# RWKV scan: backward cumulative sums by a reversed scan, backward inverse's second orientation by a mirrored TensorE product

## The chip, the cores and the metric

One core of one Trainium2 chip. The metric is the device time of one execution in microseconds (us), the median of several runs. All data are fp32.

## The reference

Two requests (1024 and 256 tokens, 1024 channels, 16 heads of 64) go through two layers with shared weights: neighbourhood attention with a gated feed-forward part, then bidirectional RWKV-7 time mixing with another. The change lies in the second mixer. In it, for each direction z (forward, and backward on the flipped sequence) and each head, a 64x64 state S runs over the tokens, and y of both directions is summed:

```python
def _wkv7_step(S, inp):
    r_t, w_t, k_t, v_t, aa_t, bb_t = inp
    sa = jnp.einsum('zbhij,zbhj->zbhi', S, aa_t)
    S = S * w_t[..., None, :] + sa[..., :, None] * bb_t[..., None, :] + v_t[..., :, None] * k_t[..., None, :]
    y = jnp.einsum('zbhij,zbhj->zbhi', S, r_t)
    return S, y
```

## The kernel before

The kernel is a sequence of stages, each with its own buffers and a barrier at its end. The change touches one of them, `rwkv_scan` (from about 2430 to 3440 us of the profile). It cuts the 1280 tokens into chunks of C = 64 and works in groups of U = 4 chunks, that is W = 256 tokens, for one pair of heads (128 partitions, one head on each half) and both directions z = 0 (forward) and z = 1 (backward). There are 8 pairs x 5 groups = 40 groups.

Within a chunk the recurrence becomes matrices. For each group: loads (SyncE); low-rank products (`lora`) and gates; running sums of the decay's logarithm over each chunk (`sums`, `sums_back`), exponentials of them on ScalarE (`exps`), keys and queries scaled by them on VectorE (`keys`, `queries`) and GpSimd (`directions`, `receptance`); products among them (`gram`), masked by VectorE (`strict_out`, `value_out`, `inclusive_out`); the inverse of a triangular 64x64 matrix for each chunk, head and direction; then the four steps of the state itself (`x_product`, `u_product`, `s_product`, each with a copy on ScalarE or, for the state, L2035 on VectorE), and the outputs (`y_products`).

**The sums.** For z = 0 a scan over the row, set to zero where a chunk begins by a multiplier `restart`, gives sums up to each token (L1910). For z = 1 the sums run from a chunk's end to each token: `sums` scans forward into `run` (L1911), and `sums_back` turns that round: it copies the chunk's total to column 0 (L1916) and subtracts the running sum from the total for the others (L1917). The semaphore `d_cum` then releases ScalarE's exponentials and GpSimd's L2085.

**The inverse** is built by doubling in levels 0 to 4 (INV = 5). Two matrices are held, `tf` and its transpose `rf`. A level is: product P of the masked matrix `bl` with `tf` (`level_p`, L1636) into `p_ps[z]`; a copy of it to `pt` by ScalarE (L1825); product T of `rf` and `pt` (`level_t`, L1647, last level L1649) into `t_ps[z]`; its sum with half of the columns of `tf` by VectorE (L2018); and then, so that `rf` follows, a VectorE transpose of the whole of `tf` in 32x32 blocks (L1993 for z = 0; L1995 for z = 1, in two instructions, because the backward inverse has the heads on swapped halves of the partitions in `rf`: `side(h, 1)` is the other half). The last level writes `rf` straight away (L2023).

Which half of the partitions a product reads and which it writes decides which quarter of the 128x128 array it works in. Forward P and T read and write the same half; backward P (`rows = halves[h]`, out `side(h, 1)`) and backward T, levels 0 to 3, read one half and write the other.

**The order** is written out by hand. Each engine runs, for I = -3 to 39, a loop over 12 slots n = 0 to 11; iteration I does the state's steps of group I, the inverse of group I + 1, the gram products of group I + 2 and the gates, sums and exponentials of group I + 3. In slot n of TensorE `inverse(I + 1, n)` does P of one direction and T of the other, interleaved chunk by chunk: in even slots 2k P forward of level k and T backward of level k - 1, in odd slots 2k + 1 P backward and T forward of level k:

```python
                    for s in range(U):
                        for h in range(2):
                            if does_p:
                                last_p = level_p(G, zp, k, s, h)
                        for h in range(2):
                            if does_t:
                                last_t = level_t(G, 1 - zp, kt, s, h)
```

State step products stand ahead of it: x, u and s in turn (n mod 3 = 0, 1, 2), and among them gram (n = 0, 1, 3, 6), lora (2), y of the group before (4, 5), turns of keys and values (7 to 10) and bonus (11). On VectorE a slot's order is: state (n = 2, 5, 8, 11), gram's masks, `level_out(I + 1, n)` (the sum and the transpose of the T product just made), and then the rest: `sums` in slot 3, `sums_back` in slot 4, `inverse_init` in 5 and 9, `keys` in 10, `queries` in 11. GpSimd runs its own row: masks of the levels (`levels`, L2117) for z = 0, then `directions` (L2085, L2087), which waits for `d_cum`, `receptance`, then the masks for z = 1. The program of every engine is written out in full for all 40 groups; there is no loop on the chip in this stage.

A 64x64 fp32 product leaves two records in the trace and two weight loads.

Of the kernel before, what the change touches and what calls it, by code (L numbers as in the profile page):

```python
# [15 lines left out]
ALU = mybir.AluOpType  # L16
# [3 lines left out]
P = 128  # L20
# [1360 lines left out]
C = 64  # L1381
# [7 lines left out]
def halves_of_level(t, z, k, other=False):  # L1389

    n = 2 ** (k + 1)
    return t.rearrange("p (b h n) -> p b h n", h=2, n=n)[:, :, (1 - z) if other else z, :]


def strided(a, off, dims):

    return bass.AP(tensor=a.tensor, offset=a.offset + off, ap=[list(a.ap[0])] + [list(d) for d in dims])


def rwkv_scan(nc, rkvl, kks, w0, w2, a0, a2, k_a, r_k, ysc, bsc, consts):  # L1400

    U = 4
    W = U * C
    NS = T // W
    NG = PAIRS * NS
    INV = LEVELS - 1
    halves = (slice(0, HD), slice(HD, P))
    with Phase(nc, "sc") as ph:
# [11 lines left out]
        restart = ph.sb("restart", [P, W])  # L1420
# [8 lines left out]
        sg = ph.sb("sg", [P, Z, W])  # L1429
# [2 lines left out]
        kd = ph.sb("kd", [P, Z, W])  # L1432
        ab = ph.sb("ab", [P, Z, W])
        cum = ph.sb("cum", [P, Z, W])
        run = ph.sb("run", [P, W])
        exb = ph.sb("exb", [P, Z, U, C + 1])
        ex2 = ph.sb("ex2", [P, Z, W])
        tb = ph.sb("tb", [P, Z, W])
# [9 lines left out]
        tf = ph.sb("tf", [P, 2, Z, U, C])  # L1448
        rf = ph.sb("rf", [P, 3, Z, U, C])
        r0 = ph.sb("r0", [P, U, C])  # L1450
        pt = ph.sb("pt", [P, Z, U, C])
# [14 lines left out]
        p_ps = [b[:, 0:256] for b in inv_ps]  # L1466
# [10 lines left out]
        a_tanh, a_sg, a_kdp, a_nega, a_ex1, a_ex2, a_x, a_u, a_fade = (  # L1477
            ph.sem(x) for x in ("a_tanh", "a_sg", "a_kdp", "a_nega", "a_ex1", "a_ex2", "a_x", "a_u", "a_fade"))
        a_pt, a_turn = ph.sems("a_pt", Z), ph.sems("a_turn", Z)
        d_start, d_cum, d_run, d_tb, d_rec, d_bonus, d_two, d_st, a_y = (  # L1480
            ph.sem(x) for x in ("d_start", "d_cum", "d_run", "d_tb", "d_rec", "d_bonus", "d_two", "d_st", "a_y"))
        d_bm, d_gram, d_first, d_t, d_r = (ph.sems(x, Z) for x in ("d_bm", "d_gram", "d_first", "d_t", "d_r"))
        g_kd, g_ab, g_r, g_bt = (ph.sem(x) for x in ("g_kd", "g_ab", "g_r", "g_bt"))
        g_bl, g_high, g_r0, g_first = (ph.sems(x, Z) for x in ("g_bl", "g_high", "g_r0", "g_first"))
# [7 lines left out]
        def group(G):  # L1492
            return 0 <= G < NG

        def side(h, z):
            return halves[h] if z == 0 else halves[1 - h]
# [8 lines left out]
        with nc.Block() as block:  # L1505
# [58 lines left out]
            def _(pe):  # L1564
# [74 lines left out]
                def level_t_waits(G, z, k):  # L1639
                    pe.wait_ge(a_pt[z], 5 * G + k + 1)  # L1640
                    if k:
                        pe.wait_ge(d_r[z], 4 * G + k)

                def level_t(G, z, k, s, h):
                    rows = side(h, z)
                    if k < INV - 1:
# [2 lines left out]
                    return nc.tensor.matmul(t_ps[z][rows, s * C:(s + 1) * C], pt_last[rows, z, s], rf[rows, G % 3, z, s],  # L1649
                                            start=True, stop=True)  # L1650

                def inverse(G, n):
                    if not group(G) or n > 2 * INV:
                        return
                    k, odd = divmod(n, 2)
                    zp = 1 if odd else 0
                    kt = k if odd else k - 1
                    does_p, does_t = k < INV, kt >= 0
                    if does_t:
                        level_t_waits(G, 1 - zp, kt)  # L1660
                    if does_p:
                        level_p_waits(G, zp, k)
                    for s in range(U):
                        for h in range(2):
                            if does_p:
                                last_p = level_p(G, zp, k, s, h)
                        for h in range(2):
                            if does_t:
                                last_t = level_t(G, 1 - zp, kt, s, h)
                    if does_p:  # L1670
                        last_p.then_inc(pe_p[zp], 1)
                    if does_t:
                        last_t.then_inc(pe_t[1 - zp], 1)

# [68 lines left out]
                for I in range(-3, NG):  # L1743
                    for n in range(3 * U):
                        s, part = divmod(n, 3)
# [144 lines left out]
            def _(dve):  # L1890
# [15 lines left out]
                def sums(G):  # L1906
                    dve.wait_ge(a_sg, G + 1)
                    if G >= 1:
                        dve.wait_ge(a_ex1, G)
                    nc.vector.tensor_tensor_scan(cum[:, 0], restart[:], sg[:, 0], 0.0, ALU.mult, ALU.add)  # L1910
                    nc.vector.tensor_tensor_scan(run[:], restart[:], sg[:, 1], 0.0, ALU.mult, ALU.add).then_inc(d_run, 1)  # L1911

                def sums_back(G):
                    dve.wait_ge(d_run, G + 1)
                    back, ahead = (t.rearrange("p (u n) -> p u n", n=C) for t in (cum[:, 1], run[:]))
                    nc.vector.tensor_copy(back[:, :, 0:1], ahead[:, :, C - 1:C])  # L1916
                    nc.vector.tensor_tensor(back[:, :, 1:C], ahead[:, :, C - 1:C].to_broadcast([P, U, C - 1]),  # L1917
                                            ahead[:, :, 0:C - 1], ALU.subtract).then_inc(d_cum, 1)

                def bonus_rows(G):  # L1920
                    p = G // NS
# [66 lines left out]
                def flat(t):  # L1988
                    return t.rearrange("p s n -> p (s n)")

                def turn_t(G, z):
                    if z == 0:
                        return nc.vector.transpose(flat(rf[:, G % 3, z]), flat(tf[:, G % 2, z]))  # L1993
                    for h, rows in enumerate(halves):
                        last = nc.vector.transpose(flat(rf[side(h, z), G % 3, z]), flat(tf[rows, G % 2, z]))  # L1995
                    return last

                def inverse_init(G, z):
                    dve.wait_ge(g_r0[z], G + 1)
                    if z == 0:  # L2000
                        nc.vector.transpose(flat(tf[:, G % 2, z]), flat(rf[:, G % 3, z])).then_inc(d_first[z], 1)
                        return
                    nc.vector.transpose(flat(tf[:, G % 2, z]), flat(r0[:])).then_inc(d_start, 1)
                    dve.wait_ge(d_start, G + 1)
                    if G >= 3:
                        dve.wait_ge(pe_u, 4 * G - 8)
                    turn_t(G, z).then_inc(d_first[z], 1)

                def level_out(G, n):
                    z = 1 - n % 2  # L2010
                    k = (n - 1) // 2
                    if not group(G) or not 0 <= k < INV:
                        return
                    dve.wait_ge(pe_t[z], 5 * G + k + 1)
                    if k < INV - 1:
                        src = halves_of_level(t_ps[z], z, k)
                        half = halves_of_level(flat(tf[:, G % 2, z]), z, k)
                        nc.vector.tensor_tensor(half, src, half, ALU.add).then_inc(d_t[z], 1)  # L2018
                        dve.wait_ge(d_t[z], 5 * G + k + 1)
                        turn_t(G, z).then_inc(d_r[z], 1)  # L2020
                    else:
                        half = rf[:, G % 3, z, :, (1 - z) * 32:(2 - z) * 32]
                        nc.vector.tensor_tensor(half, t_ps[z].rearrange("p (s n) -> p s n", s=U)[:, :, (1 - z) * 32:(2 - z) * 32], half, ALU.add).then_inc(d_t[z], 1)  # L2023

# [14 lines left out]
                for I in range(-3, NG):  # L2039
                    for n in range(3 * U):  # L2040
                        s, part = divmod(n, 3)
                        if group(I) and part == 2:
                            state_out(4 * I + s)
                        if n == 1 and group(I + 2):
                            strict_out(I + 2, 0)
                        if n == 2 and group(I + 2):
                            inclusive_out(I + 2, 0)
                        if n == 6 and group(I + 2):
                            strict_out(I + 2, 1)
                        if n == 7 and group(I + 2):  # L2050
                            inclusive_out(I + 2, 1)
                        level_out(I + 1, n)
                        if n == 0 and group(I + 2):
                            bonus_out(I + 2)
                        if n == 1 and group(I + 2):
                            value_out(I + 2, 0)
                        if n == 3 and group(I + 3):
                            sums(I + 3)
                        if n == 4 and group(I + 3):
                            sums_back(I + 3)  # L2060
                        if n == 5 and group(I + 2):
                            inverse_init(I + 2, 0)
                        if n == 6 and group(I + 2):
                            value_out(I + 2, 1)
                        if n == 8 and group(I + 3):
                            bonus_rows(I + 3)
                        if n == 9 and group(I + 2):
                            inverse_init(I + 2, 1)
                        if n == 10 and group(I + 3):
                            keys(I + 3)  # L2070
                        if n == 11 and group(I + 3):
                            queries(I + 3)
# [387 lines left out]
```

## Time and profile before

| | us |
|---|---|
| median of 3 runs | 4687.72 (4685.37 to 4695.64) |
| span of the profiled execution | 4696.3 |
| the profiled execution's own time | not listed apart from the three runs; the longest of them is 4695.64 |
| TensorE (PE) busy | 4245.7 (90%) |
| VectorE (DVE) busy | 1984.2 (42%) |
| ScalarE (ACT) busy | 1371.1 (29%) |
| GpSimd (POOL) busy | 1288.5 (27%) |

These are sums over all stages. PE is the product part of TensorE, PEld its weight loads, which overlap. The ends of products are modelled, so that a busy PE isn't one at its peak. The prediction reads the scan's steady part, 2560 to 3340 us, apart from the others.

### The profile page before, as it was taken

How to read it: one execution, taken by the hardware profiler on the slowest of the kernel's cores; microseconds unless marked ns; L12 is line 12 of the kernel's file. 1: busy time of each engine (PE TensorE's matmuls, PEld its weight loads, DVE VectorE, ACT ScalarE, POOL GpSimd, SP SyncE). 2: the span in 40 equal slices, each digit the busy share in tenths (PEclk: the TensorE clock that was granted, in tenths of full speed). 3: DMA queues.
4: the chain of work that ended last, by engine and by line, in shares of the span. 5: the costliest groups of instructions: out<-in, count | busy, mean ns of one | idle time of the engine just before them, and what ended most of it. 6: DMA issues, size and time to landing. Idle time of an engine off the chain costs nothing. (4 is left out here: it accounts for less than half of the span.)

```text
span 4696.3 us, 111143 instructions
## 1 busy us (share of the span) xinstructions
PE 4245.7 (90%) x49144; PEld 3578.0 (76%) x49144; DVE 1984.2 (42%) x3557; ACT 1371.1 (29%) x2872; POOL 1288.5 (27%) x882
## 2 busy tenths in 40 slices
PE   5999798999999997997958888888878999999997
PEld 5888666888888886775747777777756888888886
DVE  4111163253252442117227877887733253242441
ACT  2111274211110112236215555555522211111110
POOL 3111132311111124210116665665502311111110
PEclk8999899999999998998979999999988999999998
DMA  4122243312213112221232222222132312313114
GB/s 124 56 61 70 85 119 81 98 37 73 92 36 117 50 59 84 71 76 42 83 89 70 77 77 77 77 77 74 47 138 80 103 36 70 97 36 110 57 54 164
DMA packets 401484, 367.08 MB, mean 78 GB/s; under 512 B 62928, under 2 KB 370384, under 8 KB 398832
## 3 DMA queue, kind: packets, MB, share of 16 engines
q1 hardware_dynamic: 399568, 354.75, 24.6%
q8 instruction: 389, 6.37, 0.6%
q10 hardware_dynamic: 1440, 5.24, 0.3%
q14 instruction: 87, 0.71, 0.1%
HBM read 252.44 MB, written 107.48 MB: 77 GB/s over the span
## 5 line engine op out<-in xcount | busy, mean ns | idle before, releaser
L448 POOL TENSOR_TENSOR f_wlow<-f_raw,f_whigh 128x1024 fp32r<-128x1024 f32 (+1 forms) x152 | 360.4, 2371 | 1670.7 <-ACT f_whigh L519 1670.7
L504 PE MATMUL f_ps<-fx_hh,f_whigh 128*128 128x512 f32 (+1 forms) x2112 | 529.2, 359 | 0.0
L504 PE MATMUL f_ps<-fx_hl,f_whigh 128*128 128x512 f32 (+1 forms) x2112 | 528.2, 358 | 0.0
L504 PE MATMUL f_ps<-fx_hh,f_wlow 128*128 128x512 f32 (+1 forms) x2112 | 527.8, 358 | 0.0
L519 ACT ACTIVATE f_whigh<-f_raw 128x1024 fp32r<-128x1024 f32 (+1 forms) x152 | 156.5, 1030 | 922.1 <-PE f_ps L504 895.5
L504 PEld LDWEIGHTS f_ps<-fx_hl,f_whigh 128*128 128x128 f32 x2112 | 348.3, 188 | 66.2
L504 PEld LDWEIGHTS f_ps<-fx_hh,f_whigh 128*128 128x128 f32 x2112 | 348.2, 188 | 65.9
L504 PEld LDWEIGHTS f_ps<-fx_hh,f_wlow 128*128 128x128 f32 x2112 | 348.0, 188 | 66.1
L504 PE MATMUL f_ps<-mo_oh,f_whigh 128*128 128x512 f32 (+1 forms) x1440 | 361.0, 359 | 25.6 <-POOL f_wlow L448 25.6
L504 PE MATMUL f_ps<-mo_ol,f_whigh 128*128 128x512 f32 (+1 forms) x1440 | 360.4, 359 | 0.0
L504 PE MATMUL f_ps<-mo_oh,f_wlow 128*128 128x512 f32 (+1 forms) x1440 | 360.2, 358 | 0.0
L573 DVE TENSOR_TENSOR f_xo<-f_ps,f_xo 128x512 f32<-128x512 f32 x168 | 90.7, 595 | 618.8 <-PE f_ps L504 587.0
L1636 PE MATMUL sc_inv_ps<-sc_tf,sc_bl 64*64 64x64 f32 x6400 | 294.0, 226 | 26.6 <-issue 13.9
L2117 POOL TENSOR_TENSOR sc_bl<-sc_bm,sc_m_level 128x512 f32<-128x512 f32 (+1 forms) x160 | 245.7, 1557 | 231.3 <-DVE sc_pc L1940 231.3
L504 PEld LDWEIGHTS f_ps<-mo_oh,f_whigh 128*128 128x128 f32 x1440 | 240.5, 189 | 68.9 <-POOL f_wlow L448 26.2
L1636 PEld LDWEIGHTS sc_inv_ps<-sc_tf,sc_bl 64*64 64x64 f32 x6400 | 243.6, 135 | 47.3 <-issue 43.2
L504 PEld LDWEIGHTS f_ps<-mo_oh,f_wlow 128*128 128x128 f32 x1440 | 240.3, 188 | 42.8
L504 PEld LDWEIGHTS f_ps<-mo_ol,f_whigh 128*128 128x128 f32 x1440 | 240.1, 188 | 43.0
L1232 PE MATMUL ri_ps<-ri_xh,ri_whigh 128*128 128x512 f32 (+1 forms) x672 | 186.0, 387 | 74.5 <-DVE ri_xl L1348 73.5
L1647 PE MATMUL sc_inv_ps<-sc_pt,sc_rf 64*64 64x64 f32 x5120 | 228.5, 225 | 24.8 <-issue 24.7
L1647 PEld LDWEIGHTS sc_inv_ps<-sc_pt,sc_rf 64*64 64x64 f32 x5120 | 190.0, 136 | 26.6 <-issue 26.6
L594 DVE TENSOR_TENSOR f_gp<-f_ps,f_rs 128x1024 f32<-128x1024 f32 x44 | 53.9, 1226 | 357.0 <-PE f_ps L504 327.4
(267 smaller groups left out, 8482.2 us busy)
## 6 DMA issues: line engine op xcount, KB each, us to landing
f_xo<-xres SPq DMA_DIRECT2D x64, 640.0 KB
xres<-f_xo SPq DMA_DIRECT2D x56, 640.0 KB
f_raw<-in_ffn_w_gate SPq DMA_DIRECT2D x44, 512.0 KB
f_raw<-in_ffn_w_up SPq DMA_DIRECT2D x44, 512.0 KB
sc_rk<-rkvl SPq DMA_DIRECT2D x80, 256.0 KB
rkvl<-ri_ot SPq DMA_DIRECT2D x28, 640.0 KB, 2.9
f_raw<-in_ffn_w_down SPq DMA_DIRECT2D x32, 448.0 KB
qkv_raw<-in_na_w_qkv SPq DMA_DIRECT2D x24, 512.0 KB, 5.9
```

The source lines that it names most:

```text
L448: nc.gpsimd.tensor_tensor(wlow[:, m % 2, 0:kt], raw[:, 0:kt], whigh[:, m % 2, 0:kt].bitcast(F32), ALU.subtract).then_inc(cut_lo, 1)
L504: last = nc.tensor.matmul(ps[:, m % 2, n, 0:count], w[:, m % 2, k], x[:, k, t0:t0 + count], start=(k == 0 and w is whigh and x is xh), sto ...
L519: nc.scalar.activation(whigh[:, m % 2, 0:kt], raw[:, 0:kt], ACT.Copy).then_inc(cut_hi, 1)
L573: last = nc.vector.tensor_tensor(dst, src, old, ALU.add)
L594: nc.vector.tensor_tensor(gp[:, 1:1025], flat(s), rs[:, 0:1024], ALU.mult)
L1232: last = nc.tensor.matmul(ps[:, m % 2, q, 0:count], w[:, m % 2, k], src[:, k, t0:t0 + count], start=(k == 0 and w is whigh and src is xh), ...
L1636: return nc.tensor.matmul(p_ps[z][side(h, z), s * C:(s + 1) * C], bl[rows, G % 2, z, k, s], tf[rows, G % 2, z, s], start=True, stop=True)
L1647: return nc.tensor.matmul(t_ps[z][halves[h], s * C:(s + 1) * C], rf[rows, G % 3, z, s], pt[rows, z, s], start=True, stop=True)
L2117: nc.gpsimd.tensor_tensor(bl[:, G % 2, z, k:k + ks], src, mask, ALU.mult).then_inc(done[z], 1)
```

## The change

The sums of the backward direction are made by one scan that reads `sg[:, 1]` and writes `cum[:, 1]` from the last column to the first; both scans now stand in VectorE's slot 4. `run`, its semaphore, the copy and the subtraction go.

In the inverse, `rf` of the backward direction at levels 0 to 3 is no longer made by transposing `tf`. TensorE makes the transposed T product too: `level_mirrored` has the operands of `level_t` in the other order and writes the half from which it reads, into `p_ps[0]`, which is free in odd slots. It is interleaved with backward P one slot after that T (odd slots 3, 5, 7, 9), and the forward T products follow behind, by themselves. VectorE adds the result to half of the columns of `rf` (`mirrored_out`), which counts up `d_r[1]`; it stands behind the forward sum of that slot, or, at the last level, ahead of it.

```diff
@@ sums
-                    nc.vector.tensor_tensor_scan(run[:], restart[:], sg[:, 1], 0.0, ALU.mult, ALU.add).then_inc(d_run, 1)
-
-                def sums_back(G):
-                    dve.wait_ge(d_run, G + 1)
-                    back, ahead = (t.rearrange("p (u n) -> p u n", n=C) for t in (cum[:, 1], run[:]))
-                    nc.vector.tensor_copy(back[:, :, 0:1], ahead[:, :, C - 1:C])
-                    nc.vector.tensor_tensor(back[:, :, 1:C], ahead[:, :, C - 1:C].to_broadcast([P, U, C - 1]),
-                                            ahead[:, :, 0:C - 1], ALU.subtract).then_inc(d_cum, 1)
+                    back, ahead = (strided(t[:], 2 * W - 1, [[-1, W]]) for t in (cum, sg))
+                    nc.vector.tensor_tensor_scan(back, restart[:], ahead, 0.0, ALU.mult, ALU.add).then_inc(d_cum, 1)
@@ TensorE
+                def level_mirrored(G, s, h):
+                    rows = side(h, 1)
+                    return nc.tensor.matmul(p_ps[0][rows, s * C:(s + 1) * C], pt[rows, 1, s], rf[rows, G % 3, 1, s], start=True, stop=True)
...
-                    does_p, does_t = k < INV, kt >= 0
+                    does_p, does_t, does_mirrored = k < INV, kt >= 0, odd and k >= 1
...
                         for h in range(2):
-                            if does_t:
+                            if does_mirrored:
+                                last_p = level_mirrored(G, s, h)
+                            elif does_t:
                                 last_t = level_t(G, 1 - zp, kt, s, h)
                     if does_p:
                         last_p.then_inc(pe_p[zp], 1)
+                    if does_mirrored:
+                        for s in range(U):
+                            for h in range(2):
+                                last_t = level_t(G, 1 - zp, kt, s, h)
                     if does_t:
                         last_t.then_inc(pe_t[1 - zp], 1)
@@ VectorE
+                def mirrored_out(G, k):
+                    src = halves_of_level(p_ps[0], 1, k, True)
+                    half = halves_of_level(flat(rf[:, G % 3, 1]), 1, k, True)
+                    nc.vector.tensor_tensor(half, src, half, ALU.add).then_inc(d_r[1], 1)
...
                         nc.vector.tensor_tensor(half, src, half, ALU.add).then_inc(d_t[z], 1)
-                        dve.wait_ge(d_t[z], 5 * G + k + 1)
-                        turn_t(G, z).then_inc(d_r[z], 1)
+                        if z == 0:
+                            if k:
+                                mirrored_out(G, k - 1)
+                            dve.wait_ge(d_t[z], 5 * G + k + 1)
+                            nc.vector.transpose(flat(rf[:, G % 3, z]), flat(tf[:, G % 2, z])).then_inc(d_r[z], 1)
                     else:
+                        if z == 0:
+                            mirrored_out(G, k - 1)
...
-                        if n == 3 and group(I + 3):
+                        if n == 4 and group(I + 3):
                             sums(I + 3)
-                        if n == 4 and group(I + 3):
-                            sums_back(I + 3)
```

## Rows read from the trace of the kernel before

**Rows 1.** The page: span, then busy time of each engine, share, instructions.
```profile
span 4696.3 us, 111143 instructions
...
PE 4245.7 (90%) x49144; PEld 3578.0 (76%) x49144; DVE 1984.2 (42%) x3557; ACT 1371.1 (29%) x2872; POOL 1288.5 (27%) x882
```

**Rows 2.** Table by stretches, the scan's steady part; columns in the first line.
```profile
core 0: us, PE busy (x) PEld busy (x) DVE busy (x) ACT busy (x) POOL busy (x), PEclk, DMA share, GB/s
2560.00:3340.00 780.00, 659.07 (x24317) 605.36 (x24316) 621.00 (x1604) 441.57 (x1299) 467.68 (x414) 0.99 0.26 76
```

**Rows 3.** Waits of PE, 2560 to 3340 us: total, times, longest.
```profile
PE sc_inv_ps L1647 <- issue: 19.8, 20, 2.9
...
PE sc_chain_ps L1683 <- DVE sc_st L2035: 9.8, 23, 0.9
...
PE sc_inv_ps L1636 <- DVE sc_tf L2018: 4.9, 12, 1.2
...
PE sc_low_ps L1615 <- ACT sc_yt L1859: 3.5, 15, 0.2
```

**Rows 4.** Timeline of PE: start, duration, instruction, [idle before <- releaser].
```profile
2804.16 0.22 PE L1647 MATMUL sc_inv_ps<-sc_pt,sc_rf 64*64 64x64 f32 x1
2807.28 0.37 PE L1647 MATMUL sc_inv_ps<-sc_pt,sc_rf 64*64 64x64 f32 x1 [2.90 <-issue]
```

**Rows 5.** DMA queue 8 (packets, MB, share), 2560 to 3340, then 3025 to 3035.3.
```profile
q8 instruction: 193, 3.16, 1.7%
...
q8 instruction: 4, 0.07, 2.2%
```

**Rows 6.** POOL and DVE timelines: L2117 pair, four successive L1910; then all L1910 (ns, starts).
```profile
2997.63 3.04 POOL L2117 TENSOR_TENSOR sc_bl<-sc_bm,sc_m_level 128x512 f32<-128x512 f32 x2
...
2998.93 2.28 DVE L1910 TENSOR_TENSOR_SCAN sc_cum<-sc_restart,sc_sg 128x256 f32<-128x256 f32 x1 [0.17 <-ACT sc_sg L1796]
...
3022.20 2.29 DVE L1910 TENSOR_TENSOR_SCAN sc_cum<-sc_restart,sc_sg 128x256 f32<-128x256 f32 x1 [0.17 <-ACT sc_sg L1796]
...
3045.91 0.92 DVE L1910 TENSOR_TENSOR_SCAN sc_cum<-sc_restart,sc_sg 128x256 f32<-128x256 f32 x1 [0.17 <-ACT sc_sg L1796]
...
3069.53 0.92 DVE L1910 TENSOR_TENSOR_SCAN sc_cum<-sc_restart,sc_sg 128x256 f32<-128x256 f32 x1 [0.17 <-ACT sc_sg L1796]
...
L1910 DVE TENSOR_TENSOR_SCAN sc_cum<-sc_restart,sc_sg x33: 691/924/2299, 2568.3 to 3337.3; 128x256 f32<-128x256 f32 x33
```

**Rows 7.** Groups of DVE lines, 2560 to 3340: xcount | busy us, mean ns | idle.
```profile
L1995 DVE STREAM_TRANSPOSE sc_rf<-sc_tf 64x256 f32<-64x256 f32 x324 | 142.5, 440 | 7.7
...
L2018 DVE TENSOR_TENSOR sc_tf<-sc_inv_ps,sc_tf 128x128 f32<-128x128 f32 x260 | 74.6, 287 | 68.9 <-PE sc_inv_ps L1647 60.1
...
L1910 DVE TENSOR_TENSOR_SCAN sc_cum<-sc_restart,sc_sg 128x256 f32<-128x256 f32 x33 | 44.5, 1347 | 5.5 <-ACT sc_sg L1796 5.5
...
L1911 DVE TENSOR_TENSOR_SCAN sc_run<-sc_restart,sc_sg 128x256 f32<-128x256 f32 x33 | 21.8, 659 | 0.0
...
L1917 DVE TENSOR_TENSOR sc_cum<-sc_run 128x252 f32<-128x252 f32 x32 | 13.3, 414 | 0.0
...
L1916 DVE COPY sc_cum<-sc_run 128x4 f32<-128x4 f32 x32 | 5.5, 172 | 1.0
```

**Rows 8.** Timeline of PE: P and T interleaved, then a T alone.
```profile
2995.69 0.27 PE L1636 MATMUL sc_inv_ps<-sc_tf,sc_bl 64*64 64x64 f32 x2
...
2996.16 0.23 PE L1647 MATMUL sc_inv_ps<-sc_pt,sc_rf 64*64 64x64 f32 x2
2996.20 0.30 PE L1683 MATMUL sc_chain_ps<-sc_vt,sc_ga 64*64 64x64 f32 x8
...
2996.44 0.71 PE L1594 MATMUL sc_gram_ps<-sc_rec 64*64 64x128 f32 x10
...
3011.92 0.63 PE L1649 MATMUL sc_inv_ps<-sc_rf,sc_pt_last 64*64 64x64 f32 x16
3012.38 0.40 PE L1705 MATMUL sc_chain_ps<-sc_vt,sc_t 64*64 64x64 f32 x8
```

More of the change, by code:

```diff
@@ L1434, in rwkv_scan @@
         cum = ph.sb("cum", [P, Z, W])
-        run = ph.sb("run", [P, W])
         exb = ph.sb("exb", [P, Z, U, C + 1])
@@ L1479, in rwkv_scan @@
         a_pt, a_turn = ph.sems("a_pt", Z), ph.sems("a_turn", Z)
-        d_start, d_cum, d_run, d_tb, d_rec, d_bonus, d_two, d_st, a_y = (
-            ph.sem(x) for x in ("d_start", "d_cum", "d_run", "d_tb", "d_rec", "d_bonus", "d_two", "d_st", "a_y"))
+        d_start, d_cum, d_tb, d_rec, d_bonus, d_two, d_st, a_y = (
+            ph.sem(x) for x in ("d_start", "d_cum", "d_tb", "d_rec", "d_bonus", "d_two", "d_st", "a_y"))
         d_bm, d_gram, d_first, d_t, d_r = (ph.sems(x, Z) for x in ("d_bm", "d_gram", "d_first", "d_t", "d_r"))
@@ L1989, in flat @@
                     return t.rearrange("p s n -> p (s n)")
[L1991 to L1996, printed above, removed]
                 def inverse_init(G, z):
@@ L2006, in inverse_init @@
                         dve.wait_ge(pe_u, 4 * G - 8)
-                    turn_t(G, z).then_inc(d_first[z], 1)
+                    for h, rows in enumerate(halves):
+                        last = nc.vector.transpose(flat(rf[side(h, z), G % 3, z]), flat(tf[rows, G % 2, z]))
+                    last.then_inc(d_first[z], 1)
+                def mirrored_out(G, k):
+                    src = halves_of_level(p_ps[0], 1, k, True)
+                    half = halves_of_level(flat(rf[:, G % 3, 1]), 1, k, True)
+                    nc.vector.tensor_tensor(half, src, half, ALU.add).then_inc(d_r[1], 1)
                 def level_out(G, n):
```

## Prediction

> **What bounds the kernel now.** I read the page first [rows 1]: the span is 4696.3 us and TensorE is the busiest engine, but over stages of very different kinds. The change touches only the scan, so next came the table by stretches, cut to the scan's steady part [rows 2]: of 780 us TensorE is busy 659.07, VectorE 621.00 (80%), ScalarE 441.57, GpSimd 467.68. TensorE's clock is full there (0.99). Which engine sets the pace can't be read from 84% against 80%, so the third view was the waits of TensorE [rows 3]. Its idle time is 780 - 659.07 = 120.9 us. VectorE ends only 9.8 + 4.9 = 14.7 us of that, ScalarE 3.5; nearly all the rest, some 102 us, is "issue", idle time behind which no semaphore stands. One such stall is shown [rows 4]: in the middle of a row of identical products TensorE stops 2.90 us and then goes on.
>
> What is behind "issue" the DMA view tells [rows 5]: queue 8 brings instructions, 193 packets (3.16 MB, 16 KB each) in the 780 us, one each 780/193 = 4.04 us. The two halves of TensorE's work, products and weight loads, are 24317 + 24316 records in the same stretch [rows 2], 252 per packet: the packets are TensorE's own program, which is written out in full in this stage. In the densest stretch that I found, 10.3 us, four packets start; three intervals in about 10.3 us is 3.4 us each. Supply at its fastest is thus only some 15% above what the steady part draws. So two things bound this stage: the array's own time, and how quickly its instructions arrive. VectorE is busy, but TensorE seldom waits for it.
>
> A test of that is in the trace already [rows 6]. The forward scan of VectorE (L1910) takes 2.28 us where it starts while GpSimd multiplies at L2117 (from 2997.63 for 3.04 us), and 0.92 us elsewhere. This costs VectorE 1.4 us in two of five groups, and the groups don't feel it: after the two slow scans the next one starts 23.27 and 23.71 us later, after a quick one 23.62 us later. If VectorE set the pace, the first two would be over a microsecond longer.
>
> **The change part by part, per group of 4 chunks; the scan has 40.** In the steady part L1910 stands 33 times between 2568.3 and 3337.3 [rows 6]: 769.0/32 = 24.0 us a group.
>
> 1. *Removed, VectorE:* the eight 64x256 transposes of the backward inverse, two for each of its levels 0 to 3, 8 x 0.440 = 3.52 us [rows 7] (the 324 of that row are 10 a group; two belong to the start and stay). Forward transposes stay.
>
> 2. *Added, VectorE:* four sums `mirrored_out`, in operands like L2018's, 128x128 out of PSUM, 0.287 us [rows 7]: 4 x 0.29 = 1.15 us.
>
> 3. *Sums:* copy and subtraction go, about 0.17 + 0.41 us [rows 7], and the second scan stays but reads and writes backwards. No row shows a reversed scan. Bounds: as quick as the forward one, 0.659 us, and, as the bad end, 2.28 us as when the forward one met GpSimd. I take 0.66, being nearest in form. Both scans move one slot later, behind the backward sum of that slot and past the second L2117 multiply in most groups, so the 1.4 us collision should mostly go. VectorE altogether sheds 3.52 + 0.58 - 1.15 = 2.95 us a group, some 3.4 with the collision (the mean of L1910 is 1.347 us against a quick 0.92), 118 to 136 us over the stage. What waits for the sums is ScalarE's exponentials and GpSimd's L2085. The old chain ended with the subtraction in that same slot; two scans of 1.3 us take the place of transposes, copy and subtraction (0.89 + 0.58), so they end no later. I cost this at nothing; if it fails, GpSimd's slack before it is eaten first.
>
> The Trainium skill ("SBUF — State Buffer", the part on port contention) says that a VectorE instruction with two SBUF inputs and a GpSimd instruction that reads SBUF shut each other out for a whole instruction. The slow and the quick scan above agree with it; by it the subtraction's removal takes one more such meeting away, which changes VectorE's time only.
>
> 4. *Added, TensorE:* in slots 3, 5, 7, 9 eight 64x64 products `level_mirrored`, 32 a group, 1280 in all; each leaves two products and two weight loads in the records, 128 instructions a group. The price depends on which part of the array they occupy. In an odd slot today backward P reads one half of the partitions and writes the other, while forward T keeps to its own: the four quarters of the array work together. A timeline shows such a slot [rows 8]: 32 records from 2995.69, and x starts at 2996.20, 0.51 us. A set of 8 products that stands alone, backward T of the last level, has 16 records and the next product starts 12.38 - 11.92 = 0.46 us later [rows 8]. So half the work alone costs as much as two sets interleaved. In the new slot P is interleaved with the mirrored product, which keeps to its own half and so takes T's place beside P for free, and forward T follows by itself: +0.46 us in each of four slots, 1.84 us a group, 40 x 1.84 = 74 us. The other way to price it, by supply: 128 instructions are half a packet, at 3.4 us each 1.7 us a group, 68 us. The two aren't added: the lone T runs at a pace at which supply keeps up. Nor does "issue" time absorb it, as the slot draws both more time and more instructions. I take 74 and keep 0 (absorbed whole) and 2 x 74 = 148 (the mirrored product doesn't run beside P either) as outer bounds.
>
> The Trainium skill says otherwise on supply ("Runtime: NRT & Kernel Launch", Instruction fetch mechanics): crossing a 16 KiB boundary costs one DMA tail-bump, "mostly hidden". The 2.90 us stall speaks against that here. By that page the 68 us would be 0 and the 74 us of the array would stand alone.
>
> 5. *Moved and newly waited for:* backward R (`d_r[1]`) is done one slot later. In the following even slot TensorE waits for forward sum and then the mirrored sum, 0.29 us more than for the forward sum. Queued behind that wait are both products of the slot and all that follows. Cover: between the forward T and the next inverse step TensorE has x, y, gram or turn products, which hold it past that point (an x product takes 0.30 and half a gram 0.71 us [rows 8]); so nothing. If the cover is gone, 4 x 0.29 x 40 = 46 us. On VectorE the forward transpose and then the state (L2035) stand behind the new sum, 0.29 us later, but 0.89 us of transposes ahead of them are gone.
>
> 6. *Gained on TensorE:* at most what VectorE makes it wait, 14.7 us in 33 groups [rows 3], 18 for 40. I take 14, since the x products of slot 0 wait for a state that stands behind `keys`, which the change leaves.
>
> No DMA issue is added or moved on SP or GpSimd. **Sum:** +74 - 14 = +60 us. The profiled execution, 4696.3 us of span, would become 4756; it lies 8.6 us (0.2%) above the median of the runs shown, 4687.7, so the forecast is 4687.7 + 60 = 4748 us.
>
> **The rivals.**
> - *VectorE paces the scan after all* (faster). Place: the stretch from the scans to the state of slot 5, where its queue is fullest; it decides if the "issue" time is really a late VectorE. If a third of the 118 us that it sheds reaches the end and TensorE's addition runs in the cover, that is -40: 4648 us. For it: 80% busy. Against: 14.7 us of waits, and groups with slow scans are no longer. 0.14.
> - *The stalls absorb it.* 102 us of "issue" in the steady part is 3.1 us a group, more than the 1.84 added. If these stalls are fixed in time and not tied to how many instructions pass, the addition disappears in them, and 14 us may come back: 4674 to 4698, about 4688. The skill's page above would point here. Against: about six packets a group are drawn, and half a one more has to come too. 0.13.
> - *Dearer than costed.* The new wait of 5 decides as well, from the point at which the cover of 0.3 us is missing: 60 + 46 = +106, 4794 us; or the mirrored set doesn't pair with P, toward +134. Against: rows 8 show that pairing for the same halves. 0.11.
> - *Forecast:* 0.62.
>
> **How the numbers follow.** A measurement here can tell about 0.2%, 9 us. Faster takes the first rival and a little of the second: 0.16. Same is most of the second: 0.11. Slower: 0.73. The forecast's own range is +35 to +80, 4723 to 4768. For 8 in 10 I go down to the second rival's 4684 and up to 4782, part of the way to the dear case; left out are the faster case below and the rest of the dear one above.
>
> **What would show it.** Right: TensorE has 51704 product records in the whole kernel instead of 49144 (1280 x 2 more); VectorE some 118 us less busy; L1910's slow cases gone; the distance from scan to scan near 25.6 us instead of 24.0; 6.4 instruction packets a group; T records after P and mirrored ones, taking 0.46 us alone. Wrong: a distance of 24 us or less with "issue" shrunken; waits of the P product for `sc_rf` from the mirrored sum (the dear case); waits of L2085 grown beyond 102 us would show the sums late.

## The result, and the profile after

The changed kernel takes 4755.18 us (median of 4 runs, 4753.37 to 4755.74) against 4686.55 us, 68.6 us more: a ratio of 1.0142, interval 1.0129 to 1.0154. The forecast was 4748, in the range 4684 to 4782, with 0.73 on slower. The size came out. Why it is this size the prediction had only half right, and the experiments correct it.

The page after, its span and busy times:

```profile
span 4753.7 us, 116023 instructions
...
PE 4297.4 (90%) x51704; PEld 3637.5 (77%) x51704; DVE 1817.2 (38%) x3317; ACT 1373.3 (29%) x2872; POOL 1288.5 (27%) x882
```

Beside [rows 1]: 2560 more product records, as counted, and VectorE 1984.2 - 1817.2 = 167.0 us less busy. So VectorE lost more work than forecast, and the kernel became slower. The same stretch of the scan as in [rows 2], in the same columns, and then the packets of queue 8 (packets, MB, share), in that stretch and in the whole:

```profile
2560.00:3340.00 780.00, 662.91 (x24669) 616.54 (x24665) 451.03 (x1315) 415.38 (x1215) 439.51 (x390) 0.99 0.24 72
```

```profile
q8 instruction: 195, 3.19, 1.7%
...
q8 instruction: 409, 6.70, 0.6%
```

VectorE's 621.00 us have become 451.03. TensorE draws 195 packets of instructions in 780 us where it drew 193 [rows 5]: its program arrives as quickly as before, one packet each 4.0 us, but there is more of it. The kernel before drew 389 packets in all; 20 more for 40 groups are the half a packet a group of the prediction. How long a group takes can be read from the first of its scans, now L1919 (duration in ns min/median/max, first and last start), with the reversed one, L1921:

```profile
L1919 DVE TENSOR_TENSOR_SCAN sc_cum<-sc_restart,sc_sg x30: 680/681/1115, 2568.1 to 3315.7; 128x256 f32<-128x256 f32 x30
L1921 DVE TENSOR_TENSOR_SCAN sc_cum<-sc_restart,sc_sg x30: 658/666/669, 2568.7 to 3316.2; 128x256 f32<-128x256 f32 x30
```

747.6/29 = 25.78 us a group, against 24.03 [rows 6]: 1.75 us more, 70 us for 40 groups, all of the difference. The reversed scan costs what the forward one did (0.666 and 0.659 us), and the slow meetings with GpSimd are gone: the longest L1919 here is 1.115 us, where ten of the 33 in [rows 6] took 2.17 us or more.

The waits of TensorE (total, times, longest), and how VectorE's groups stand (xcount | busy us, mean ns | idle before, releaser):

```profile
PE sc_inv_ps L1635 <- issue: 18.6, 17, 1.7
PE sc_inv_ps L1646 <- issue: 15.0, 17, 2.3
...
PE sc_inv_ps L1653 <- issue: 10.3, 12, 1.9
...
PE sc_chain_ps L1692 <- DVE sc_st L2043: 4.8, 13, 0.4
```

```profile
L2021 DVE TENSOR_TENSOR sc_tf<-sc_inv_ps,sc_tf 128x128 f32<-128x128 f32 x244 | 71.3, 292 | 224.6 <-PE sc_inv_ps L1646 216.9
...
L2010 DVE TENSOR_TENSOR sc_rf<-sc_inv_ps,sc_rf 128x128 f32<-128x128 f32 x121 | 34.3, 284 | 42.3 <-PE sc_inv_ps L1648 42.3
```

TensorE's waits for VectorE shrank from 14.7 us [rows 3] to 4.8. VectorE now stands idle 216.9 us ahead of the sums of T (L2021) until TensorE's products are there; ahead of L2018 it was 60.1 [rows 7]. The relieved engine waits over three times as long as before for the one that took the work.

A slot with the mirrored products, in a timeline of TensorE: L1635 is P, L1653 the mirrored product, L1646 the forward T, L1706 the u product of the next slot.

```profile
2901.42 0.22 PE L1653 MATMUL sc_inv_ps<-sc_rf,sc_pt 64*64 64x64 f32 x2
2901.44 0.27 PE L1635 MATMUL sc_inv_ps<-sc_tf,sc_bl 64*64 64x64 f32 x2
2901.47 0.28 PE L1653 MATMUL sc_inv_ps<-sc_rf,sc_pt 64*64 64x64 f32 x4
...
2901.88 0.57 PE L1646 MATMUL sc_inv_ps<-sc_pt,sc_rf 64*64 64x64 f32 x14
2902.24 0.27 PE L1706 MATMUL sc_chain_ps<-sc_xs,sc_rf 64*64 64x64 f32 x2
```

The mirrored products run among the P products in the time that T had, and T follows alone: 0.36 us until the next slot's product begins, against the 0.46 reckoned (in most slots of the stage it is between 0.36 and 0.47).

### The profile page after: what moved, and what is told of

Same layout as the page of the kernel before. It is cut to its first block and busy times, and to the rows that moved or that the text cites. A ratio compares the mean times of both kernels' runs of the same rounds, so it can differ in the third digit from the quotient of the medians.

```text
span 4753.7 us, 116023 instructions
## 1 busy us (share of the span) xinstructions
PE 4297.4 (90%) x51704; PEld 3637.5 (77%) x51704; DVE 1817.2 (38%) x3317; ACT 1373.3 (29%) x2872; POOL 1288.5 (27%) x882
## 5 line engine op out<-in xcount | busy, mean ns | idle before, releaser
L1635 PE MATMUL sc_inv_ps<-sc_tf,sc_bl 64*64 64x64 f32 x6400 | 295.7, 226 | 25.5 <-issue 22.8
L1635 PEld LDWEIGHTS sc_inv_ps<-sc_tf,sc_bl 64*64 64x64 f32 x6400 | 244.0, 135 | 41.5 <-issue 38.2
L1646 PE MATMUL sc_inv_ps<-sc_pt,sc_rf 64*64 64x64 f32 x5120 | 224.4, 224 | 19.6 <-issue 19.6
L2021 DVE TENSOR_TENSOR sc_tf<-sc_inv_ps,sc_tf 128x128 f32<-128x128 f32 x320 | 93.4, 292 | 292.3 <-PE sc_inv_ps L1646 282.8
L1646 PEld LDWEIGHTS sc_inv_ps<-sc_pt,sc_rf 64*64 64x64 f32 x5120 | 186.6, 135 | 23.1 <-issue 23.1
```

Source lines behind the costliest of these rows:

```text
L1635: return nc.tensor.matmul(p_ps[z][side(h, z), s * C:(s + 1) * C], bl[rows, G % 2, z, k, s], tf[rows, G % 2, z, s], start=True, stop=True)
L1646: return nc.tensor.matmul(t_ps[z][halves[h], s * C:(s + 1) * C], rf[rows, G % 3, z, s], pt[rows, z, s], start=True, stop=True)
```

## The experiments

The theory was that TensorE pays, in array time or in supply of instructions; the rivals were that VectorE sets the pace, and that the new wait costs. Each kernel is compared with the kernel before on the same chip (medians 4701.29, 4698.20 and 4705.36 in the three sets).

### The parts of the change, each alone

**Sums alone** (the reversed scan in slot 4, the inverse as before):

```diff
-                    nc.vector.tensor_tensor_scan(run[:], restart[:], sg[:, 1], 0.0, ALU.mult, ALU.add).then_inc(d_run, 1)
...
+                    back, ahead = (strided(t[:], 2 * W - 1, [[-1, W]]) for t in (cum, sg))
+                    nc.vector.tensor_tensor_scan(back, restart[:], ahead, 0.0, ALU.mult, ALU.add).then_inc(d_cum, 1)
```

> The kernel before with the reversed scan a slot later, the inverse as before. TensorE's own time pays (theory): VectorE loses about 1.0 us a group (0.59 us of copy and subtraction, 0.43 us of collisions with GpSimd) and the end hardly moves: 0 to -8 us, 4678 to 4687. VectorE paces the scan (rival): a third or more of the 40 us that VectorE sheds comes through, -13 us or beyond, below 4674. The later sums hurt (rival): the exponentials and L2085 start late, +9 us or more.

Measured: 4698.71 against 4701.29 us, 0.9990 (0.9979 to 1.0001). VectorE is 42 us less busy by the page (1941.9), and nothing that can be measured comes through.

**Inverse alone** (the changed kernel with the sums of before):

```diff
+                def sums_back(G):
+                    dve.wait_ge(d_run, G + 1)
...
-                        if n == 4 and group(I + 3):
+                        if n == 3 and group(I + 3):
                             sums(I + 3)
+                        if n == 4 and group(I + 3):
+                            sums_back(I + 3)
```

> The changed kernel with the old sums. TensorE pays (theory): nearly the whole difference stands here, +60 to +80 us against the kernel before, 4746 to 4767. If the moved sums were the cause (rival), this kernel is within 15 us of the kernel before.

Measured: 4772.25 against 4701.29 us, +71.0, 1.0152 (1.0136 to 1.0168). The whole price is in the inverse. Against the 1.0142 of the whole change the sums give back 0.1% of the time, which lies inside the intervals.

**Relief alone** (VectorE spared the backward transposes, TensorE's work the same):

```diff
-                    if k:
+                    if k and z == 0:
                         pe.wait_ge(d_r[z], 4 * G + k)
...
-                        turn_t(G, z).then_inc(d_r[z], 1)
+                        if z == 0:
+                            turn_t(G, z).then_inc(d_r[z], 1)
```

> The kernel before without the transposes of the backward inverse at levels 0 to 3 (L1995, 8 of its 10 a group) and without TensorE's wait for them: the backward matrix R is left at its first value, so the inverse of the backward direction is another. TensorE's products stay as many. Theory: VectorE sheds 3.5 us a group, 141 us, and the end gains only what TensorE waits for VectorE, 5 to 18 us: 4668 to 4681. VectorE paces (rival): -40 us or more, below 4647.

Measured: 4694.40 against 4701.29 us, -6.9, 0.9987 (0.9978 to 0.9996), at the near end of the theory. VectorE is 130.9 us less busy over the kernel (1984.2 to 1853.3 by the pages), and 7 us of that arrive. The rival in which VectorE sets the pace, -40 us or more, is out.

**Products alone** (as many products as the change adds, in the same places and on the same halves, but from constants, so that nothing new is waited for; VectorE keeps its work):

```diff
+                def level_mirrored(G, s, h):
+                    rows = side(h, 1)
+                    return nc.tensor.matmul(p_ps[0][rows, s * C:(s + 1) * C], m_level[rows, 0, 0], ident[rows, rows], start=True, stop=True)
...
+                            if does_mirrored:
+                                last_p = level_mirrored(G, s, h)
...
+                    if does_mirrored:
+                        for s in range(U):
+                            for h in range(2):
+                                last_t = level_t(G, 1 - zp, kt, s, h)
```

> The kernel before with 32 products more a group in the places and the array half of the mirrored ones, from constants, their result unused, and forward T alone behind them as in the change. VectorE keeps all its work. Theory: the whole price without VectorE's relief, +70 to +90 us, 4756 to 4777, at or above the changed kernel. Rival (the price is the new wait for the mirrored sum, which is absent here): under +35 us.

Measured: 4766.27 against 4701.29 us, +65.0, 1.0137 (1.0121 to 1.0152), 5 us under the band. It is not the new wait: without it nearly the whole price is there. By this kernel and relief alone, inverse alone should be +58; it is +71. The 13 us between may be the new wait or the spread of layout and runs (the intervals are 7 us to either side); this is not settled.

**The change as a whole, again**, with the kernels of the last set, so that they share a chip:

> The changed kernel itself, beside the others of this set on one chip: +64 to +73 us against the kernel before, as measured first. It stands here so that it can be compared with the kernel of small added products, which costs 61.

Measured: 4773.71 against 4705.36 us, +68.4, 1.0142 (1.0127 to 1.0158).

### Array time or supply

Both prices of the prediction's step 4 gave about 70 us, so their sizes can't tell them apart. **Small** adds 32 products of 8 columns a group, **wide** adds 8 of 256 columns, both in slots 3, 5, 7, 9 ahead of P and T:

```diff
+                    if odd and k >= 1:
+                        for s in range(U):
+                            for h in range(2):
+                                nc.tensor.matmul(p_ps[0][halves[h], s * C:s * C + 8], ident[halves[h], halves[h]], m_level[halves[h], 0, 0, 0:8],
+                                                 start=True, stop=True)
```

```diff
+                    if odd and k >= 1:
+                        for h in range(2):
+                            nc.tensor.matmul(p_ps[0][halves[h], 0:256], ident[halves[h], halves[h]],
+                                             m_level[halves[h], 0:2].rearrange("p a z n -> p (a z n)"), start=True, stop=True)
```

> The kernel before with 32 products of 8 columns more a group in slots 3, 5, 7, 9 (128 instructions), ahead of P and T, which stay interleaved; results unused. Array time is paid (theory A): 8 columns cost an eighth of 64, some 0.06 us a slot at most, under +15 us. Instruction supply is paid (theory B): half a packet a group at 3.4 us, +50 to +70 us, as much as the change. Both bind in turn: in between, 20 to 45.

> The kernel before with two products of 256 columns more in each of the same slots, one on each half: the array time of eight 64-column ones (0.43 to 0.46 us a slot) with a quarter of their instructions (32 a group). Array time is paid (theory A): +60 to +74 us. Supply is paid (theory B): an eighth of a packet a group, 0.4 us, +10 to +25 us. Both in turn: in between.

Measured: small 4759.09 against 4698.20 us, +60.9, 1.0133 (1.0117 to 1.0148); wide 4717.49, +19.3, 1.0039 (1.0025 to 1.0053). What each puts into a slot, from timelines of TensorE, small first:

```profile
2903.68 0.41 PE L1666 MATMUL sc_inv_ps<-sc_m_level,sc_ident 64*64 64x8 f32 x10
...
2904.06 0.20 PE L1666 MATMUL sc_inv_ps<-sc_m_level,sc_ident 64*64 64x8 f32 x1
```

```profile
2899.08 0.38 PE L1665 MATMUL sc_inv_ps<-sc_m_level,sc_ident 64*64 64x256 f32 x1
...
2899.09 0.38 PE L1665 MATMUL sc_inv_ps<-sc_m_level,sc_ident 64*64 64x256 f32 x1
...
2899.30 0.38 PE L1665 MATMUL sc_inv_ps<-sc_m_level,sc_ident 64*64 64x256 f32 x2
...
2899.51 0.22 PE L1649 MATMUL sc_inv_ps<-sc_rf,sc_pt_last 64*64 64x64 f32 x2
```

The expectation of small was wrong in one point: products of 8 columns are not an eighth as dear. Sixteen records start from 2903.68 to 2904.06, each about as far from the next as those of 64 columns; their weight loads are as long as ever (135 ns). So small doesn't separate array time from instructions by itself. The pair does: both kernels keep their quarters of the array for about 0.4 us a slot (0.38 and 0.43), and they differ in instructions, 128 and 32 a group. The price follows the instructions: 61 and 19 us. At small's rate 32 instructions cost 61/4 = 15 us, which leaves wide 4 us for 4 x 0.43 x 40 = 69 us of array time. Array time is nearly free here, because TensorE is waiting for its program in any case. The steady part of wide, in the columns of [rows 2], shows where it goes:

```profile
2560.00:3340.00 780.00, 687.00 (x24133) 628.76 (x24133) 599.17 (x1560) 429.26 (x1265) 455.64 (x406) 0.99 0.25 74
```

TensorE is 27.9 us longer busy than before with nearly as many records, and its "issue" time fell from 100.4 to 82.4 us: the wide products fill time in which it stood idle.

That "issue" time is a wait for instructions can be read from the traces themselves. From 2560 to 3340 us of the changed kernel TensorE has 94 gaps of more than 0.5 us in which neither a product nor a weight load runs. Every one ends between 1.0 and 1.75 us after the landing of the last packet of queue 8 before it (median 1.39); with a packet each 4.0 us chance would put about one gap in five there. In small it is 98 of 98, in wide 70 of 70, in the kernel before 81 of 89, and in the kernel with one product of y, where VectorE holds TensorE up (below), 39 of 81. The distance from one packet's start to the next is not even: in the steady part of the kernel before it goes from 3.3 to 7.0 us, with 3.9 in the middle. What sets it, no run here shows.

**Twice as many small products**: the same edit with `for s in range(2 * U)`.

> Twice as many 8-column products in each of slots 3, 5, 7, 9: 256 instructions a group more than the kernel before. If how many instructions TensorE gets sets the pace (supply), the price doubles from the 61 us of 128: +115 to +130 us, and the packets in 780 us stay near 193. If the 61 us came from something that happens once a slot (a wait, the order of P behind other products, a switch of bank), it stays near 61, under 80.

Measured: 4855.08 against 4705.36 us, +149.7, 1.0318 (1.0304 to 1.0332). More than twice, so it is nothing that happens once a slot; the band was too low. The 28 us above twice 61 aren't explained; the clock of the stretch was 0.97 here and 0.99 before, which may be a part of them. The scan of this kernel and its packets, 2560 to 3340 us:

```profile
L1915 DVE TENSOR_TENSOR_SCAN sc_cum<-sc_restart,sc_sg x27: 691/693/1379, 2584.7 to 3314.9; 128x256 f32<-128x256 f32 x27
```

```profile
q8 instruction: 192, 3.15, 1.7%
```

730.2/26 = 28.08 us a group, 4.05 us more than before for one packet more. That is one packet at the mean distance, 780/192 = 4.06 us, and not at the 3.4 of the densest stretch. By the measured times, over all 40 groups, a packet costs 60.9/20 = 3.0 us in small and 149.7/40 = 3.7 us here.

**Fewer**: y from two of its three products, and from one. The first leaves the values' own part out of y, the second also the part of the state's corrections; all else is done.

```diff
-                                nc.tensor.matmul(y_ps[side(h, z), z, to[z]], tu[rows, g, z], nr[rows, G % 4, z, 0, s], start=False, stop=False)
-                        for h, rows in enumerate(halves):
-                            for z in range(Z):
-                                last = nc.tensor.matmul(y_ps[side(h, z), z, to[z]], vt[rows, G % 2, z, s], nr[rows, G % 4, z, 1, s], start=False, stop=True)
+                                last = nc.tensor.matmul(y_ps[side(h, z), z, to[z]], tu[rows, g, z], nr[rows, G % 4, z, 0, s], start=False, stop=True)
```

> The kernel before without the third of the three products that make y (the values' own part), 16 products and 64 instructions a group fewer, 0.25 packets. Supply: -30 us (-22 to -35), by 61 us for 128 instructions. Array time (16 products in four quarters, 0.23 us a group): -9 us. VectorE paces: 0 to -5.

> The kernel before with one of the three products of y, 128 instructions a group fewer: the change's addition with the other sign. Supply, still alone: -55 to -65 us, 4640. Supply until VectorE, which keeps all its work (19 us busy a group of 24), takes over as the next limit: -35 to -50. Array time: -18 us.

Measured: two products 4677.56 against 4705.36 us, -27.8, 0.9939 (0.9925 to 0.9952); one product 4661.03, -44.3, 0.9907 (0.9892 to 0.9922). The first 64 instructions give 28 us, in supply's band and three times the array time of those products. The next 64 give 16.5. What has taken over, the waits of TensorE and the packets of the kernel with one product tell:

```profile
PE sc_inv_ps L1636 <- DVE sc_tf L2012: 34.7, 39, 2.2
PE sc_chain_ps L1683 <- DVE sc_st L2029: 34.1, 51, 0.9
PE sc_low_ps L1724 <- issue: 5.9, 6, 1.9
```

```profile
q8 instruction: 183, 3.00, 1.6%
```

VectorE now ends 68.8 us of TensorE's idle time, where it was 14.7 [rows 3], "issue" has shrunk from 100.4 to 31.2 us, and packets come more rarely than they could, 183. With two products it is 34.8 and 75.5 us: VectorE comes in as the next limit step by step, within 44 us of the kernel before. That the work which this change takes from VectorE would be worth something below that point follows from it, but no run shows it.

### An attempt to use it

Transposes of `turn` for the lower half of the partitions were issued as transposes (the other stages' form, one record and one weight load each) in the hope of 48 instructions a group fewer; once alone, once with the sums:

```diff
+                def turned(out, a, rows):
+                    if rows.start == 0:
+                        return nc.tensor.transpose(out, a, ident[rows, rows])
+                    return nc.tensor.matmul(out, a, ident[rows, rows], start=True, stop=True)
```

> The kernel before with the turns of keys and values on the lower half of the partitions issued as transposes, one product record and one weight load instead of two of each, so 24 x 2 = 48 instructions a group fewer; the upper half, at its side in the array, is as before. Supply binds (theory B): 48/128 of the 68 us reckoned for 128 instructions, -15 to -26 us. Array time binds (theory A): 0 to -5 us. VectorE paces: 0.

> The reversed scan a slot later together with those transposes. If supply binds, what the transposes give plus what the sums alone give, -15 to -35 us: faster than both kernels. If array time alone binds: within 9 us of the kernel before.

Measured: 5126.72 against 4698.20 us, 1.0912 (1.0897 to 1.0927), and with the sums 5135.59, 1.0918 (1.0899 to 1.0937). A clear miss in both. The turns of this kernel (L1601 the transposes, L1602 the products), first at full clock, then at half, then those of the kernel before (L1615 and L1618, the granted clock full), and the steady part of this kernel in the columns of [rows 2]:

```profile
2890.66 0.24 PE L1601 MATMUL sc_low_ps<-sc_ident,sc_rec 64*64 64x64 f32 x1
2890.83 0.32 PE L1602 MATMUL sc_low_ps<-sc_ident,sc_rec 64*64 64x64 f32 x2
2891.08 0.24 PE L1601 MATMUL sc_low_ps<-sc_ident,sc_rec 64*64 64x64 f32 x1
...
2899.84 0.31 PE L1601 MATMUL sc_gram_ps<-sc_ident,sc_rec 64*64 64x64 f32 x1
2900.08 0.47 PE L1602 MATMUL sc_gram_ps<-sc_ident,sc_rec 64*64 64x64 f32 x2
2900.48 0.31 PE L1601 MATMUL sc_gram_ps<-sc_ident,sc_rec 64*64 64x64 f32 x1
```

```profile
2890.38 0.40 PE L1615 MATMUL sc_gram_ps<-sc_ident,sc_rec 64*64 64x64 f32 x8
2890.61 0.28 PE L1618 MATMUL sc_gram_ps<-sc_ident,sc_vb 64*64 64x64 f32 x4
2890.73 0.40 PE L1615 MATMUL sc_gram_ps<-sc_ident,sc_rec 64*64 64x64 f32 x8
2890.96 0.28 PE L1618 MATMUL sc_gram_ps<-sc_ident,sc_vb 64*64 64x64 f32 x4
2891.08 0.40 PE L1649 MATMUL sc_inv_ps<-sc_rf,sc_pt_last 64*64 64x64 f32 x6
```

```profile
2560.00:3340.00 780.00, 729.90 (x16249) 592.89 (x16249) 426.82 (x1107) 306.17 (x897) 324.06 (x288) 0.79 0.18 54
```

A transpose and a product on different quarters hardly overlap: each starts when the other is nearly done. A pair takes 0.43 us where the granted clock is 1.0 and 0.64 where it is 0.5, against (2891.08 - 2890.38)/6 = 0.12 us for two products before. Half of the 24 x 40 = 960 pairs fell on each level, about 510 us for all, where they took 112: some 400 of the 428 us lost. The granted clock fell to 0.79 in this stretch, where the kernel before had 0.99. How much of the loss is the clock's no run separates. TensorE's product records thinned from 24317 to 16249 in the 780 us. No version here is clearly faster than the kernel before.

## Why the prediction was right, and where its reason was off

*What bounds the stage* held. VectorE at 80% busy was not the limit: relief alone sheds 131 us of its work and brings 7. The test by slow and quick scans pointed the same way. That "two things bound this stage", the array's own time and the arrival of instructions, was too even-handed: supply binds, and the array has slack. Two readings on the way were a little off and change nothing: 4.04 us against 3.4 is 19% and not 15%, and the slow scans are ten of 33 and not two in five.

*Steps 1 and 2* (transposes out, sums in) held by the instruction, 0.284 us for L2010, but VectorE lost more than the 118 to 136 us forecast: 167.0. Two terms were mis-sized. One is the mirrored sum, which I counted whole. The timeline of VectorE shows that records overlap:

```profile
2902.56 0.29 DVE L2021 TENSOR_TENSOR sc_tf<-sc_inv_ps,sc_tf 128x128 f32<-128x128 f32 x1 [1.69 <-PE sc_inv_ps L1646]
2902.77 0.28 DVE L2010 TENSOR_TENSOR sc_rf<-sc_inv_ps,sc_rf 128x128 f32<-128x128 f32 x1
2902.97 0.43 DVE L2026 STREAM_TRANSPOSE sc_rf<-sc_tf 128x256 f32<-128x256 f32 x1
```

The sum starts 0.08 us before the record ahead of it ends and is itself overlapped by 0.08, so it adds 0.12 us of busy time, 0.16 less than counted, 26 us over 160. The other is the collision: I took 0.92 us for a quick scan, but undisturbed it takes 0.68, so the collisions cost 1.347 - 0.68 = 0.67 us a group and not 0.43. They haven't all gone, as some scans still take up to 1.115 us: over the 40 groups the forward scans fell from 55.2 to 30.9 us, 24 us where 17 were counted. 136 + 26 + 7 = 169 us is near the 167.0.

*Step 3* held: a reversed scan costs 0.666 us, the sums aren't late (GpSimd's waits for them, named there as the sign, are 16.2 us in the 780 and were 102.4), and the end doesn't feel them (0.9990).

*Step 4* gave the right size for a reason that is half wrong. It priced the products by array time, 0.46 us for the lone T in four slots, 74 us, and by supply, 68 us, and took the first; products alone measured 65. The pairing that it read from [rows 8] is there, but a lone 0.4 us in such a slot costs almost nothing: wide shows 19 us, 15 of them by its instructions. The term that stands is the supply of half a packet a group. Its price, 3.4 us a packet, was read at the densest stretch; the addition of the change came at 1.75/0.5 = 3.5 us a packet, two half packets together at 4.05; by the measured times 68.6/20 = 3.4, between the 3.0 of small and the 3.7 of small twice.

*Step 5*, the new wait costed at nothing: products without it cost 65 us, and in the 780 us TensorE never waits for the mirrored sum (in the whole stage 1.6 us). The 13 us that don't add up in the inverse stay open.

*Step 6*, 14 us gained, was too much: relief alone brings 6.9. The products were put 9 us too high (74 against 65) and the relief 7 too high, which made up for each other: +60 forecast, +58 by the two experiments. The other 10 us up to +68.6 are not in the sum at all. That the forecast came so near is in part luck.

*The rivals.* "The stalls absorb it" fell for the right reason: the "issue" time is tied to how many instructions pass (193, 195, 192 packets in kernels whose groups differ by 4 us, and gaps that end 1.0 to 1.75 us after a packet has landed). The Trainium skill ("Runtime: NRT & Kernel Launch", Instruction fetch mechanics) calls the cost of crossing a 16 KiB boundary "mostly hidden"; here it isn't, by the 61 us of small against the 19 of wide and by those gaps.

## What to carry to other kernels

Where a stage is written out in full with many small products, count TensorE's instructions as a resource of their own: instruction packets per unit of work against packets per microsecond, beside the "issue" time. If the packets come at nearly one rate whatever the kernel does, moving work from a VectorE that nobody waits for to TensorE costs by the instruction, and one product of 256 columns is much cheaper than four of 64 (here +19 us for wide against +65 for products alone). Ask how long the engine to be relieved is waited for (here 14.7 us in 780), not how busy it is (80%).

## What the runs showed of the hardware that I had not expected

- TensorE's instructions arrived at one 16 KB packet each 4.0 to 4.1 us on average (190 to 195 in 780 us) in the kernel before, the changed one and all with added work, with 8% and 17% more instructions too; 188 and 183 where VectorE began to hold TensorE up (y from two products and from one).
- A TensorE that has run out of instructions goes on 1.0 to 1.75 us after the next packet has landed, 1.4 in the middle (all 94 gaps of more than 0.5 us in 780 us of the changed kernel).
- A 64x64 fp32 product of 8 columns takes its quarter of the array about as long as one of 64 columns (16 records in 0.4 us); its weight load is 135 ns in both.
- Transposes and ordinary products in turn, on separate quarters, hardly overlap: 0.43 us a pair at full clock and 0.64 at half, against 0.12 for two products; the stretch's clock went from 0.99 to 0.79.
- A scan read and written backwards is as quick as a forward one, 0.666 against 0.659 us.
